# Hymba block on one core: the norm of kk applied by token in the masks and the turned keys instead of being turned and multiplied into kk

## What is computed

```python
kk = (k * k_k).reshape(B, T, H, N)
kk = kk / jnp.maximum(jnp.linalg.norm(kk, axis=-1, keepdims=True), 1e-12)
b = kk * a
def step(S, inp):
    sa = -jnp.einsum('bhvk,bhk->bhv', S, kk_t)
    S = S * w_t[:, :, None, :] + sa[..., None] * b_t[:, :, None, :] + v_t[..., None] * k_t[:, :, None, :]
    y = jnp.einsum('bhvk,bhk->bhv', S, r_t)
```

## Time and profile before

| | |
|---|---|
| median of 3 runs | 1979.27 us (1978.47 to 1979.85) |
| profiled execution, its own time | 1980.56 us |
| its span | 1978.8 us |
| TensorE matmul busy | 1922.7 us (97%) |
| VectorE busy | 1247.0 us (63%) |
| ScalarE busy | 801.3 us (40%) |
| GpSimd busy | 264.0 us (13%) |
| chain that ended last | PE 88%, DVE 5%, ACT 4%, DMA 2% |
| granted TensorE clock, mean | 0.991 |

### The profile page before, as it was taken

How to read it: one execution, slowest core, us unless ns; L and a number is a source line. 1 busy time by engine, 2 the same in 40 slices (tenths; PEclk the granted TensorE clock), 3 DMA queues, 4 the chain that set the end, 5 groups by cost and what they waited for, 6 DMA issues and landing times.

```text
span 1978.8 us, 39502 instructions
## 1 busy us (share of the span) xinstructions
PE 1922.7 (97%) x15982; PEld 1543.4 (78%) x15982; DVE 1247.0 (63%) x2352; ACT 801.3 (40%) x1566; POOL 264.0 (13%) x591
## 2 busy tenths in 40 slices
PE   8999999999999999999999999999999999999994
PEld 5777878778787877878787787878887778887883
DVE  5657576766667676675767667676767754346434
ACT  6443434353434344434343434343434443234221
POOL 0001112020202020011020202020202031111112
PEclk9999999999999999999999999999999999999997
DMA  5533232333324234332323323232323443456442
GB/s 182 177 99 89 73 100 73 95 83 85 91 80 97 76 93 153 95 94 68 99 79 88 91 81 97 76 94 74 95 81 88 155 109 107 126 175 193 156 117 107
DMA packets 208454, 207.25 MB, mean 105 GB/s; under 512 B 114960, under 2 KB 117008, under 8 KB 208272
## 3 DMA queue, kind: packets, MB, share of 16 engines
q1 hardware_dynamic: 208272, 204.73, 37.0%
HBM read 181.08 MB, written 23.59 MB: 103 GB/s over the span
## 4 chain that ended last, share of the span: by engine, by line
PE 88%; DVE 5%; ACT 4%; DMA 2%; issue 1%; DVEq 0%; POOL 0%; SPq 0%; ACTq 0%; POOLq 0%
PE psum L1109 68%; PE psum L1094 3%; PE psum L1262 2%; PE psum L1217 2%; PE psum L1243 2%; ACT score L584 2%; PE psum L1253 2%; PE psum L1178 2%; ACT w_hi L510 1%; DVE score L904 1%; PE psum L1366 1%; DVE w_lo L704 1%; PE psum L1328 1%; PE psum L1201 1%; PE psum L1162 1%
## 5 line engine op out<-in xcount | busy, mean ns | idle before, releaser
L1109 PE MATMUL psum<-x_hi,w_hi 128*128 128x512 f32 x2144 | 886.0, 413 | 10.6 <-DVE x_lo L713 7.7
L1109 PE MATMUL psum<-x_hi,w_lo 128*128 128x512 f32 x2144 | 839.4, 392 | 0.0
L1109 PE MATMUL psum<-x_lo,w_hi 128*128 128x512 f32 x2144 | 837.3, 391 | 0.0
L704 DVE TENSOR_TENSOR w_lo<-w_raw,w_hi 128x512 fp32r<-128x512 f32 x536 | 371.7, 694 | 604.7 <-ACT w_hi L510 590.1
L510 ACT ACTIVATE w_hi<-w_raw 128x512 fp32r<-128x512 f32 x536 | 335.5, 629 | 873.5 <-PE psum L1109 866.2
L1109 PEld LDWEIGHTS psum<-x_hi,w_hi 128*128 128x128 f32 x2144 | 404.1, 188 | 120.1 <-DVE w_lo L704 18.8
L1109 PEld LDWEIGHTS psum<-x_hi,w_lo 128*128 128x128 f32 x2144 | 403.4, 188 | 89.0
L1109 PEld LDWEIGHTS psum<-x_lo,w_hi 128*128 128x128 f32 x2144 | 404.8, 189 | 80.6 <-issue 8.0
L452 POOL COPY xt<-sub_ident 64x256 f32<-64x256 f32 x16 | 11.7, 728 | 1021.2 <-DMA x<-scratch_L 1021.2
L458 POOL TENSOR_TENSOR x<-x,xt 64x15 f32<-64x15 f32 (+7 forms) x240 | 87.3, 364 | 18.8
L460 POOL TENSOR_TENSOR xt<-xt,x 64x15 f32<-64x15 f32 (+7 forms) x240 | 81.5, 340 | 18.8
(11 more groups left out here) (237 smaller groups left out, 1938.8 us busy)
## 6 DMA issues: line engine op xcount, KB each, us to landing
w_raw<-in_w_in SPq DMA_DIRECT2D x408, 256.0 KB, 2.7
w_raw<-in_w_out SPq DMA_DIRECT2D x128, 256.0 KB, 2.7
stage<-in_x_t SPq DMA_DIRECT2D x20, 256.0 KB, 3.7
stage<-scratch_MIX SPq DMA_DIRECT2D x19, 256.0 KB, 4.6
scratch_L<-late SPq DMA_DIRECT2D x32, 128.0 KB, 2.6
x<-scratch_X SPq DMA_DIRECT2D x32, 128.0 KB, 3.3
x_t<-scratch_XT SPq DMA_DIRECT2D x32, 128.0 KB, 3.7
scratch_MIX<-sa SPq DMA_DIRECT2D x16, 256.0 KB, 3.1
```

Of the source, the lines that this page charges most:

```text
L704: nc.vector.tensor_tensor(w_lo[gq % SPLIT][:], w_raw[gq % RAW][:], w_hi[gq % SPLIT][:].bitcast(F32), ALU.subtract).then_inc(w_ready, 1)
L1109: mm = nc.tensor.matmul(psum[:, s % 2], wt[gq % SPLIT][:, cols], xx[:, c], start=(c == 0 and wt is w_hi and xx is x_hi), stop=(c == KC - 1 ...
```

## The change

The factor 1 / (sum of squares) is no longer multiplied into kk. It stays with the token on the partition, in a new tile `scal` (128 x 4 x 2 x 2), and is applied where the token of b is on the partition: in the masks (the rows of `am` that belong to b) and in the turned keys. The rows of k keep the factor 1.0, so the squares are written with the two chunks of each block exchanged, which puts a chunk's sums on the partitions of its b rows.

- The square on ScalarE at step 5 is two instructions of half the columns.
- The spread copy on VectorE (step 11), the four turns on TensorE (step 12) and the product into k (step 13) go; the reciprocal is two instructions of 64 partitions; the product with k_k goes into the two instructions that write `qr`.
- `masked` is 16 instructions of 128 x 128 with a scalar per partition instead of four of 128 x 512.
- The two copies of turned keys go from ScalarE to two products on VectorE at step 3, ahead of the scan, counted by a new semaphore `kbt_read`.
- Where TensorE waited for `kk_read` at step 14 it waits for `inv_ready`, and for `va_read` once.

```diff
@@ ScalarE, channels
                     if at == 5:
                         act.wait_ge(k_ready, j + 1)
-                        nc.scalar.activation(s1, k, ACT.Square, scale=p(n, "k_k")).then_inc(squares, 1)
+                        by_chunk = "p (b c t) -> p b c t"
+                        for c in range(2):
+                            ins = nc.scalar.activation(s1.rearrange(by_chunk, b=NB, c=2)[:, :, 1 - c],
+                                                       k.rearrange(by_chunk, b=NB, c=2)[:, :, c],
+                                                       ACT.Square, scale=p(n, "k_k"))
+                        ins.then_inc(squares, 1)
@@ ScalarE, recurrence
                     if at == 3:
-                        act.wait_ge(t_full, 4 * i + 1)
-                        for m in range(2):
-                            act.wait_ge(t_full, 4 * i + m + 1)
-                            copy(late[:, 4 + m], psum[:, 6 + m]).then_inc(t_read, 1)
                         act.wait_ge(t_full, 4 * i + 3)
@@ VectorE, channels
                     if at == 11:
-                        dve.wait_ge(norm_done, 2 * j + 1)
+                        dve.wait_ge(norm_done, j + 1)
                         then(nc.vector.tensor_scalar(inv2[:], psum[:, 2, 0:BH], 1e-24, None, ALU.max))
-                        then(nc.vector.reciprocal(inv2[:], inv2[:]))
-                        then(nc.vector.tensor_copy(grow.rearrange("p (m d) -> p m d", d=HD),
-                                                   inv2[:].unsqueeze(2).broadcast_to([P, BH, HD])))
+                        for c in range(2):
+                            us = us_rows(c)
+                            ins = nc.vector.reciprocal(scal[us, :, c], inv2[us].rearrange("p (b h) -> p b h", h=2))
+                        then(ins)
                         dve.sem_inc(inv_ready, 1)
                     if at == 13:
-                        dve.wait_ge(norm_done, 2 * j + 2)
-                        then(nc.vector.scalar_tensor_tensor(k, k, p(n, "k_k"), psum[:, 3], ALU.mult, ALU.mult))
+                        for c in range(2):
+                            ins = nc.vector.scalar_tensor_tensor(
+                                qr[:, :, 2 - c], k.rearrange(chunks, b=NB, c=2)[:, :, c], p(n, "k_k"),
+                                decay[:, :, 0:C].rearrange("p (b c) t -> p b c t", c=2)[:, :, c], ALU.mult, ALU.mult)
+                        then(ins)
                         dve.sem_inc(kk_read, 1)
-                        for c in range(2):
-                            ins = nc.vector.tensor_tensor(
-                                qr[:, :, 2 - c], k.rearrange(chunks, b=NB, c=2)[:, :, c],
-                                decay[:, :, 0:C].rearrange("p (b c) t -> p b c t", c=2)[:, :, c], ALU.mult)
-                        then(ins)
@@ VectorE, masked
                     for hh in range(2):
-                        bank = (6, 4)[half] + hh
-                        ins = nc.vector.tensor_tensor(
-                            am[:, 2 * half:2 * half + 2, hh].rearrange("p b c x t -> p b (c x t)"),
-                            psum[:, bank].rearrange("p (b t) -> p b t", b=2), many(const("amask"), 2), ALU.mult)
+                        for bb in range(2):
+                            for c in range(2):
+                                b, f = 2 * half + bb, 2 * bb + c
+                                ins = nc.vector.scalar_tensor_tensor(
+                                    am[:, b, hh, c].rearrange("p x t -> p (x t)"),
+                                    psum[:, (6, 4)[half] + hh, f * P:(f + 1) * P], scal[:, b, c, hh:hh + 1],
+                                    const("amask")[:, c * P:(c + 1) * P], ALU.mult, ALU.mult)
@@ VectorE, recurrence
+                    if at == 3:
+                        for m in range(2):
+                            dve.wait_ge(t_full, 4 * i + m + 1)
+                            then(nc.vector.tensor_tensor(
+                                late[:, 4 + m].rearrange("p (f d) -> p f d", d=HD),
+                                psum[:, 6 + m].rearrange("p (f d) -> p f d", d=HD),
+                                scal[:, 2 * m:2 * m + 2].rearrange("p b c h -> p (b c h)").unsqueeze(2).broadcast_to(
+                                    [P, BH, HD]), ALU.mult))
+                            dve.sem_inc(kbt_read, 1)
@@ TensorE, channels
-                    if at == 12:
-                        pe.wait_ge(inv_ready, j + 1)
-                        pe.wait_ge(sigma_a, j + 1)
-                        if j % PAIRS == 0:
-                            pe.wait_ge(va_read, j // PAIRS + 1)
-                        for b in range(NB):
-                            mm = turn(psum[:, 3, b * P:(b + 1) * P], grow[:, b * P:(b + 1) * P])
-                        mm.then_inc(norm_done, 1)
@@ TensorE, scores and step 14
-                        pe.wait_ge(t_read, 4 * i + 2)
+                        pe.wait_ge(kbt_read, 2 * i + 2)
...
-                            pe.wait_ge(kk_read, i + 2)
+                            pe.wait_ge(inv_ready, i + 2)
+                        if i == PAIRS - 1:
+                            pe.wait_ge(va_read, 2)
```

More of the change, by code:

```diff
@@ L149, in program @@
         inv2 = sb("inv2", [P, BH])
+        scal = sb("scal", [P, NB, 2, 2])
         pc = sb("pc", [P, 2, NCH])
@@ L234, in program @@
         a_full, a_read = sem("a_full"), sem("a_read")
+        kbt_read = sem("kbt_read")
         t_full, t_read = sem("t_full"), sem("t_read")
@@ L1045, in _ @@
                 nc.vector.memset(raw[:, 0:1], 0.0)
+                nc.vector.memset(scal[:], 1.0)
                 then(nc.vector.memset(keep[:], 1))
@@ L1276, in recurrence @@
                         scores(i, 0)
-                        pe.wait_ge(t_read, 4 * i + 4)
+                        pe.wait_ge(t_read, 2 * i + 2)
                         mm = from_chunks(4, lambda b, c, hh: am[vs_rows(c), b, hh, c, 1 - c],
@@ L1353, in recurrence @@
                         if i != PAIRS - 2 and i < INTERVALS - 1:
-                            pe.wait_ge(t_read, 4 * i + 7)
+                            pe.wait_ge(t_read, 2 * i + 3)
                         if i < INTERVALS - 2 and i != PAIRS - 2:
```

## The result

| | before | changed |
|---|---|---|
| median, us | 1979.56 (1978.47 to 1980.05, 4 runs) | 1998.90 (1996.61 to 2000.01, 4 runs) |
| ratio, 95% interval | | 1.0097 (1.0082 to 1.0112) |
| span of the profiled execution, us | 1978.8 | 1997.0 |

A forecast was written before the change was run, and what follows sets the result against it. TensorE's own queue was taken to bound the kernel (97% busy). First pair -1.8 us and masks +19.3 us summed to +17.5 us, so 1998.1 for the profiled execution and 1996.8 us for the median; range 1987 to 2006.

The forecast's parts named there:

- Growth of the masks: VectorE, step 1: 16 masks with a scalar take 4.56 us against 2.71 for four, 1.84 us more.
- The ends I had kept: Bounds on mask spacing: scalar free, growth 0.8 us (chance 0.07); no overlap, growth 2.9 us (chance 0.06).
- The slack of 0.50 us and the path gate, sigmoids, turns: Late masks delay gate and decay sigmoids; beyond 0.50 us slack, TensorE waits 1.34 us at the key turns in 13 intervals.
- Formula: Whole change in us: 14 times the growth of the masks, less 8.3.
- i = 0 and i = 7 pay nothing: No mask cost there: a table load covers most of it in i = 0; in i = 7 the gate shifts before the masks.
- The removed turns, booked at 0: TensorE, step 12: 0.48 us saved in each of 15 cases is spent waiting for the softmax norm, so 0.
- rival B: The 0.48 us of the turns removed at step 12 is kept, 7.2 us less, 1989.6 us; chance 0.12.
- The hold at step 13: TensorE's wait for the softmax norm at step 13 grows from 0.2 to 0.4-0.7 us.
- The first pair's 1.8 us: First head pair, step 12: without the turns a longer wait goes too, booked whole once, -1.8 us.
- The last interval: i = 15: the key turns already wait for the masks themselves and take their growth in full, +1.84 us.
- The moved keys cost nothing under TensorE's delay: Turned keys on VectorE at step 3 make the scan 1.0 us later, TensorE 1.34 us later; 0.3 us slack, cost 0.
- The L round trip at 0: L is stored after the masks, inverted by GpSimd and sent back; it loses 0.5 of 2.3 us margin, cost 0.

The follow-up runs named there:

- e3: Changed kernel with the next pair's two sigmoids (decay and a) ahead of the gate's sigmoid on ScalarE at step 2; 1985.76 us.
- e11: Kernel before with only the second half's masks as eight of 128x128 with a scalar of 1.0; 1986.83 us.
- e9: Changed kernel with the four turns of step 12 issued again on TensorE, result unused; 1998.92 us.
- e1: Changed kernel with the four 128x512 masks of before, factor left out of the masks; 1978.88 us.
- e4: Kernel before with the next pair's two sigmoids ahead of the gate's sigmoid on ScalarE; 1978.67 us.
- e7: Kernel before with the softmax norm at the front of VectorE's steps 8 and 12, ahead of the weights' low part; 1969.48 us.
- e2: Kernel before with the 16 masks of 128x128 and a scalar of 1.0, nothing else changed; 1998.36 us.
- e5: Changed kernel with the softmax norm at the front of VectorE's steps 8 and 12, ahead of the weights' low part; 1978.54 us.
- e6: Changed kernel with both reorderings: next pair's sigmoids first on ScalarE, softmax norm first on VectorE; 1964.66 us.
- e8: e3 with the turned keys copied on ScalarE as before, the 16 masks kept; 1983.46 us.
- e10: e6 with the four turns of step 12 issued again on TensorE; 1976.79 us.

## Why the prediction was right

- **Growth of the masks**, taken 1.84 us: measured 4.46 - 2.71 = 1.75. One lasts 0.343 us (0.34 taken); from (4.46 - 0.16 - 2 x 0.343) / 14 they start 0.258 us apart (0.266 taken). The ends I had kept, 0.20 and 0.34 apart, were both off; the row with the same operation and a scalar was the right neighbour. By the Trainium skill ("VectorE: DVE Perf Modes", The DRAIN you can't avoid) the next instruction starts only when the pipe is empty; here it starts 0.085 us before the last one ends. The overhead that the Trainium skill gives in "Perfetto Trace Analysis" for PSUM (about 125 ns) is near the 0.258 - 0.13 = 0.13 us that is left after 128 columns, but the four masks of before show 0.07 for it: the rest comes with the scalar.
- **The slack of 0.50 us and the path gate, sigmoids, turns**: 13 intervals of 1.34 forecast. In the changed kernel the distances from one start of the key turns to the next exceed those of before by 1.22 to 1.44 us, 16.9 us in all (17.4 forecast). e3 shows the path, e11 the slack. Formula and measured growth would give 13 x 1.25 = 16.2; the interval is 0.05 us longer than that, so the slack was 0.45.
- **i = 0 and i = 7 pay nothing**: in i = 0 the wait is 0.68 us, before 0.67, and in i = 7 it is 0.15 in both. The stretch from i = 6 to i = 7 even became 0.8 us shorter, 132.38 against 133.20, which was in no term; 0.5 of it is a shorter wait of TensorE for L850 (L847 before).
- **The removed turns, booked at 0**: right (e9), and rival B is refuted. The hold at step 13 is now 0.73 us of idle weight loading, 0.4 to 0.7 forecast.
- **The first pair's 1.8 us**: the key turns of i = 0 come at 142.22 instead of 142.74, 0.5 sooner. The matmuls of step 10 ahead of them started 1.3 us later than before (88.15 against 86.84; the first matmuls on the constants waited 0.9 us for their transfer, before not at all), so 1.8 is gained between the two. With the turns issued again in e9 1.6 of it is lost.
- **The last interval**, 1.84 forecast: it grew by 3.9 us, 98.0 to 101.9. The wait for the masks at the turns, which was to take G in full, grew only from 0.85 to 1.16. Ahead of the masks TensorE's matmuls wait 5.83 us for L850, before 3.40, in a stretch where x for the output projection is loaded and split. With the old masks the interval took 97.6 to 98.2 (e1, e4 and e7), with eight of the 16 99.9 (e11), and with the 16 in e2, e3, e5, e6, e8, e9 and e10 99.2 to 100.9: about the masks, and in the changed kernel 1 to 2.7 us of something that changes from run to run. The end of the program gave 1.2 back. Terms off by 2.0 and 1.2, neither traced further.
- **The total**: the span grew by 18.2 us where the sum was 17.5. The terms missed by -0.5 (the 13 intervals), +1.3 (the first pair, lost in the start-up), +2.0, -0.8 and -1.2, which nearly cancel. The mechanism is shown by the steady intervals; that the total came within 2.1 us is in part luck.
- **The moved keys cost nothing under TensorE's delay**: right (e1). The exponentials of the decay start 6.67 us after the key turns, 7.08 before: 0.4 of cover left, 0.3 forecast.
- **The L round trip at 0**: right for this kernel. A kernel in which TensorE does not wait at the turns loses more of the margin, and in e6 and e10 it is used up in some intervals.

## What to carry to other kernels

Before splitting an instruction on an engine that is "only 63% busy", list what stands behind it in its own queue and, from there, what the next engine has queued behind the instruction that waits: here a product, then a sigmoid, then an unrelated sigmoid that TensorE needed. Cutting work from the bounding engine pays only if what it waits for next does not start from an event ahead of the cut; move that (here the softmax norm ahead of the weights' low part in VectorE's queue) and the same cut counts. Then the slack to the next hold must be measured again, since each kernel that is faster meets a new one.

## What the runs showed that was not expected

VectorE's softmax norm (four instructions of 256 columns, scalar per partition, from and to SBUF) lasts 1.14 us in all 32 cases of the changed kernel and of e8, where GpSimd does nothing beside it, but 1.36 to 1.52 in seven of e3 and 1.54 to 1.62 in nine of e6: in all of these GpSimd's copy of 64x256 runs beside it for 0.4 us or more. The weights' low part (128x512, two inputs in SBUF) lasts 1.07 instead of 0.69 us beside the same copy (e3, i = 3, 6, 9 and 10). Beside GpSimd's small products alone (0.9 us of them) it lasts 1.18 to 1.23 in five cases of e6. The Trainium skill ("Perfetto Trace Analysis", Optimizing Scalar/DVE Operations) says that GpSimd and VectorE share a port into SBUF, which an instruction that uses both of VectorE's holds for itself; the trace agrees as far as the two meet in time, and no run here switched GpSimd off to show it.
